# Mixture-of-experts blocks of 32 rows on four column tiles in place of 64 rows on two

## The reference, cut to what matters

```python
def expert_block(args):
    xb, e = args
    g, u = jnp.split(xb @ w_gu[e], 2, axis=-1)        # (rows,1024) @ (1024,1024)
    return (jax.nn.silu(g) * u) @ w_dn[e]             # (rows,512) @ (512,1024)
...
y = ys[dest].reshape(T, TOP_K, D)
return jnp.einsum('tk,tkd->td', wts.astype(y.dtype), y)
```

## Time and profile before

| | |
|---|---|
| median of 3 runs | 2094.38 us (2094.16 to 2096.64) |
| the profiled execution | 2094.28 us, its span 2092.5 us |
| PE busy | 1722.3 us, 82% of the span |
| DVE, ACT, POOL busy | 33%, 17%, 12% |
| moved by DMA | 516.19 MB, mean 247 GB/s |
| expert stage of layer 0 | from 459.86 to 1112.32 us |
| expert stage of layer 1 | from 1461.67 to 2064.68 us |

### The profile page before, as it was taken

How to read it: one execution, slowest core, us unless ns; L and a number is a source line. 1 busy time by engine, 2 the same in 40 slices (tenths; PEclk the granted TensorE clock), 3 DMA queues, 4 the chain that set the end, 5 groups by cost and what they waited for, 6 DMA issues and landing times.

```text
span 2092.5 us, 19483 instructions
## 1 busy us (share of the span) xinstructions
PE 1722.3 (82%) x7263; PEld 763.4 (36%) x7263; DVE 689.7 (33%) x1090; ACT 354.9 (17%) x740; POOL 250.1 (12%) x242
## 2 busy tenths in 40 slices
PE   3899999869596678788886999795969888888883
PEld 2545776443132223223323444344323332323231
DVE  5286554252212322211112279875111111111112
ACT  1234442101010101111101124310111111101110
POOL 1002110021211211111100111100011101110100
PEclk9999999959898889899997999895999999999997
DMA  9065000337959888999993412033695999999985
GB/s 374 11 249 193 0 0 1 122 148 268 411 211 394 355 355 343 387 359 370 358 350 137 153 60 73 8 150 143 223 386 217 363 365 356 363 354 359 350 346 202
DMA packets 144707, 516.19 MB, mean 247 GB/s; under 512 B 14738, under 2 KB 27215, under 8 KB 141299
## 3 DMA queue, kind: packets, MB, share of 16 engines
q1 hardware_dynamic: 128912, 497.96, 61.4%
q0 software_dynamic: 13408, 16.85, 2.3%
q10 hardware_dynamic: 2306, 0.28, 0.1%
HBM read 515.03 MB, written 29.36 MB: 260 GB/s over the span
## 4 chain that ended last, share of the span: by engine, by line
PE 62%; DMA 21%; DVE 12%; issue 2%; ACT 1%; SPq 1%; POOLq 0%; DVEq 0%; POOL 0%; ACTq 0%
PE ps L932 25%; DMA ring_gu<-in_moe_w_gu_dram 19%; PE ps L945 11%; PE ps L761 3%; PE ps L866 3%; PE ps L672 3%; PE ps L788 3%; PE ps L831 2%; DVE ring_dn L1566 2%; PE ps L687 2%; PE ps L774 1%; PE ps L707 1%; DVE gate_bc L1277 1%; DMA ring_gu<-in_w_ada_dram 1%; PE ps L938 1%
## 5 line engine op out<-in xcount | busy, mean ns | idle before, releaser
L932 PE MATMUL ps<-ring_gu,arena 128*64 128x512 f32 x2816 | 700.0, 643 | 199.5 <-DMA ring_gu<-in_moe_w_gu_dram 196.0
L932 PEld LDWEIGHTS ps<-ring_gu,arena 128*64 128x64 f32 x2816 | 208.3, 147 | 619.7 <-issue 530.2
L945 PE MATMUL ps<-ring_dn,arena 128*64 128x512 f32 x1408 | 317.1, 592 | 0.9 <-ACT arena L1214 0.9
L573 POOL DMA_INDIRECT ys_dram<-arena,out_idx x88 | 126.5, 1438 | 1077.3 <-DVE arena L1753 1077.3
L1777 DVE TENSOR_TENSOR arena<-arena,ps 128x256 f32<-128x256 f32 x88 | 37.0, 421 | 588.9 <-ACT arena L1227 588.9
L1214 ACT ACTIVATE arena<-ps 128x256 f32<-128x256 f32 x88 | 33.7, 384 | 849.1 <-PE ps L938 849.1
L945 PEld LDWEIGHTS ps<-ring_dn,arena 128*64 128x64 f32 x1408 | 100.9, 137 | 201.3 <-issue 199.9
L1753 DVE SCALAR_TENSOR_TENSOR arena<-ps,wtab,gate_bc 128x512 f32<-128x512 f32 x88 | 66.0, 751 | 237.1 <-PE ps L945 237.1
L1742 DVE TENSOR_SCALAR arena<-ps,scale_col,shift_col 128x128 f32<-128x128 f32 x176 | 60.1, 403 | 223.3 <-PE ps L923 223.3
L831 PE MATMUL ps<-arena 128*128 128x512 f32 x256 | 110.6, 592 | 1.0 <-ACT arena L1070 1.0
L1206 ACT ACTIVATE arena<-ps,shift_col,scale_col 128x128 f32<-128x128 f32 x176 | 66.2, 456 | 91.2 <-PE ps L923 91.2
(11 more groups left out here) (290 smaller groups left out, 1476.8 us busy)
## 6 DMA issues: line engine op xcount, KB each, us to landing
ring_gu<-in_moe_w_gu_dram SPq DMA_DIRECT2D x64, 4096.0 KB, 18.2
ring_dn<-in_moe_w_dn_dram SPq DMA_DIRECT2D x64, 2048.0 KB, 10.1
ring_gu<-in_w_ada_dram SPq DMA_DIRECT2D x12, 2048.0 KB, 10.3
arena<-in_w_ada_dram SPq DMA_DIRECT2D x16, 1536.0 KB, 11.2
ring_dn<-ys_dram SPq DMA_DIRECT2D x8, 1024.0 KB, 7.8
arena<-in_rnn_w_in_dram SPq DMA_DIRECT2D x8, 1024.0 KB, 5.8
ring_gu<-in_mla_w_o_dram SPq DMA_DIRECT2D x1, 4096.0 KB, 19.3
xn_dram<-arena SPq DMA_DIRECT2D x2, 2048.0 KB, 18.3
```

The lines of the kernel that those rows point to most:

```text
L573: g.indirect_dma_start(ys_dram, bass.IndirectOffsetOnAxis(ap=out_idx[:, col:col + 1], axis=0), yo[:, n % 2, :], None, bounds_check=4 * SEQ ...
L932: last = mm(ps[s_ * ROWS:(s_ + 1) * ROWS, pb, :].rearrange("p (a b) -> p a b", a=2), rows[:, k, :], pair[:, :, s_, :], start=(k == 0), sto ...
L945: last = mm(ps[s_ * ROWS:(s_ + 1) * ROWS, pb, :], part, w[:, f, s_ * HALF:(s_ + 1) * HALF], start=(f == 0), stop=(f == FT - 1))
```

## The change

`ROWS` becomes 32 and there are four column tiles (`TILES`). The caps are 2, 2, 5, 4, 3, 3, 3, then 2 for nine ranks and 1 for sixteen: 56 blocks. Ranks with 1 block alternate with the larger ones in `SEQUENCE`. In `gate_up` and `down` each matmul has a 128x32 stationary and a 128x256 moving operand, four to a slice. The hidden block is 128x128, so that one transpose does; the ACT and DVE operations on it are half as long, and a row of `yo` is 256 numbers, written to `ys_dram` in rows of 256. A unit is four blocks; the first unit is gathered with one indirect DMA, each other unit with four of 32 rows. The counting of blocks and columns in DVE takes a few more operations, the building of `tok_idx` fewer.

```diff
+QUARTER = D // 4
-ROWS = 64
-CAP = [2, 2, 4] + [2] * 7 + [1] * 22
+ROWS = 32
+TILES = P // ROWS
+CAP = [2, 2, 5, 4, 3, 3, 3] + [2] * 9 + [1] * 16
+SEQUENCE = [0, 1, 16, 2, 17, 3, 18, 4, 19, 5, 20, 6, 21, 7, 22, 8, 23, 9, 24, 10, 25, 11, 26, 12, 27, 13, 28, 14, 29, 15, 30, 31]
+BLOCKS = [(_o, _j) for _o in SEQUENCE for _j in range(CAP[_o])]
...
+                    for q in range(TILES):
+                        o, j = BLOCKS[TILES * t + q]
+                        col = o + COLBASE[j]
+                        rows = slice(q * ROWS, (q + 1) * ROWS)
+                        g.indirect_dma_start(xg[rows, t % 2, :], None, xn_dram,
+                                             bass.IndirectOffsetOnAxis(ap=tok_idx[0:ROWS, col:col + 1], axis=0),
...
                     for k in ks:
-                        pair = w[:, k, :].rearrange("p (two s f) -> p two s f", two=2, s=2)
-                        for s_ in range(2):
-                            last = mm(ps[s_ * ROWS:(s_ + 1) * ROWS, pb, :].rearrange("p (a b) -> p a b", a=2), rows[:, k, :],
-                                      pair[:, :, s_, :], start=(k == 0), stop=(k == KT - 1))
+                        parts = w[:, k, :].rearrange("p (two s f) -> p two s f", two=2, s=TILES)
+                        for s_ in range(TILES):
+                            last = mm(ps[s_ * ROWS:(s_ + 1) * ROWS, pb, 0:2 * P].rearrange("p (a b) -> p a b", a=2),
+                                      rows[:, k, :], parts[:, :, s_, :], start=(k == 0), stop=(k == KT - 1))
...
-                    if half and t + 1 < NU:
+                    if q == TILES - 1 and t + 1 < NU:
                         rows_transposed(t + 1)
...
-                then(v.tensor_scalar(ncap, order, float(HEAVY), 1.0, ALU.is_lt, ALU.add))
-                then(v.tensor_scalar(ovb, order, 2.0, 2.0, ALU.is_equal, ALU.mult))
-                then(v.tensor_tensor(ncap, ncap, ovb, ALU.add))
+                then(v.tensor_scalar(ovb, order, 2.0, float(NE), ALU.is_lt, ALU.mult))
+                then(v.tensor_tensor(ovb, ovb, order, ALU.add))
+                then(v.tensor_scalar(ncap, order, 16.0, 1.0, ALU.is_lt, ALU.add))
+                for first in (7.0, 4.0, 3.0):
+                    then(v.scalar_tensor_tensor(out=ncap, in0=ovb, scalar=first, in1=ncap, op0=ALU.is_lt, op1=ALU.add))
...
-                    v.scalar_tensor_tensor(out=yo[:, n % 2, :], in0=ps[:, 5 + n % 2, :], scalar=wtab[:, col:col + 1],
-                                           in1=gate_bc[:, 1, 0:HALF], op0=ALU.mult, op1=ALU.mult
+                    v.scalar_tensor_tensor(out=yo[:, n % 2, :], in0=ps[:, 5 + n % 2, 0:QUARTER], scalar=wtab[:, col:col + 1],
+                                           in1=gate_bc[:, 1, 0:QUARTER], op0=ALU.mult, op1=ALU.mult
```

More of the change, by code:

```diff
@@ L378, in dn_rows, with rows_landed @@
             return moe_w_dn[l, e].rearrange("(k p) n -> p k n", p=P)
+        def rows_landed(l, t):
+            return sum(16 if u == 0 else 16 * TILES for m in range(l + 1) for u in range(t % 2, NU, 2) if m < l or u <= t)
         @block.sync
@@ L586, in _ @@
                         gather(t + 2)
-                    if t:
-                        scatter(2 * t - 1)
-                    scatter(2 * t)
+                    for n in range(max(TILES * t - 1, 0), TILES * t + TILES - 1):
+                        scatter(n)
                 scatter(NB - 1)
@@ L960, in block_down @@
                         pe.wait_ge(S["yo_ready"], base + n - 1)
-                    down(5 + n % 2, hmidT[:, n % 2, :, :], DN[place % 2]).then_inc(S["dn_done"], 1)
+                    down(5 + n % 2, hmidT[:, n % 2, :], DN[place % 2]).then_inc(S["dn_done"], 1)
                 pe.sem_inc(OV[l]["dn_done"], 1)
@@ L1254, in _ @@
                         else:
-                            rows = slice(hf * ROWS, (hf + 1) * ROWS)
-                            A(gate_bc[rows, 1, 0:HALF], bank(g)[rows, :], ACT.Copy).then_inc(S["a_free"], 1)
+                            for q in range(2):
+                                rows = slice((2 * hf + q) * ROWS, (2 * hf + q + 1) * ROWS)
+                                last = A(gate_bc[rows, 1, 0:QUARTER],
+                                         bank(g)[rows, q * QUARTER:(q + 1) * QUARTER], ACT.Copy)
+                            last.then_inc(S["a_free"], 1)
         @block.vector
@@ L1446, in _ @@
                 else:
-                    rows = slice((n - 2) * ROWS, (n - 1) * ROWS)
-                    v.tensor_copy(gate_bc[rows, 1, 0:HALF], bank(g)[rows, :]).then_inc(S["d_free"], 1)
+                    for q in range(2):
+                        rows = slice((2 * n - 4 + q) * ROWS, (2 * n - 3 + q) * ROWS)
+                        last = v.tensor_copy(gate_bc[rows, 1, 0:QUARTER],
+                                             bank(g)[rows, q * QUARTER:(q + 1) * QUARTER])
+                    last.then_inc(S["d_free"], 1)
             def k_out(h, hb):
```

166 lines of the change are left out of this document (80 added, 86 removed).

## The result

The changed kernel takes **2007.5 us** (median of 4 runs, 2000.95 to 2008.95), beside 2094.4 before: ratio 0.9577, 95% interval 0.9554 to 0.9600. It is 87 us faster; 157 were forecast, and the range (1895 to 2030) held. The profiled execution took 2008.95 us, its span is 2007.2.

The account below looks back on a forecast made before the run. PE's time per block was taken to make holes in DMA, which would then bound the kernel. Gains of 16 (starts), 79 (layer 1) and 64 (layer 0), less 2 (DVE counting), made 157: 2094.3 to 1937 us, range 1895 to 2030.

Parts of the forecast that it names:

- Four at once: PE in gate_up and down: four column tiles run together, by the lower value for load-matmul pairs, giving a 5.7 us block.
- Rival 3: PE's expert blocks: two tiles at a time or pairs at 0.117 us, block about 11.1 us, 2161 us, slower; chance 0.11.
- DMA as the bound, holes only at large experts: Expert stages: weight transfers set the time, with holes of 12, 6 and three of 1 us, 21; layer 0 31.
- The slow half after a wait: PE after waiting for a load: runs at the half clock level, 2 us put into each larger expert's first block.
- Start of layer 1: First load comes 9.5 us after the first matmul, where it was 17.21; gain 7.7 us.
- 478.5 of transfers: Layer 1's expert stage: DMA moves the remaining bytes at 412 GB/s in 478.5 us.
- gathers hidden: POOL in the expert stages: 53 gathers for 22 a layer, about 1 us each, fit under 500 us and cost nothing.
- The loop isn't entered.: Overflow loop behind the blocks: the token counts fit the new caps, so no time was put in for it.
- 5 us from the last landing to the end of down: End of each expert stage: a down of 1.7 us and what is left of the last hidden block, 5 us.
- The start of layer 0: First load comes 9.5 us after the first matmul, where it was 18.04; gain 8.5 us.
- rival 2: PE's expert blocks: four tiles overlap only in part, block 8.5 to 9 us, 2010 to 2020 (1975 to 2060); chance 0.20.
- dearer scatters: Scatter rows of 1 KB in place of 2 KB: 12 us in both layers if dearer, kept only for the range.

Follow-up runs that it names:

- number 10: Number 9 with its one gather of 128 rows split again into four of 32, POOL's wait and DVE's copies kept; 1960.3 us.
- 11: number 10 without POOL's wait for DVE's column, the DVE copies kept but unused; 1972.0 us.
- Number 6: The changed kernel with fewer slices in gate_up and down from an expert's third block on, all loads kept, part of the computation left out; 1977.4 us.
- Number 9: The changed kernel with the overflow loop skipped by one outer condition and one gather of 128 rows per unit in place of four; 1934.2 us.
- number 1: The changed kernel with MAX_EXTRA, the trips of the empty overflow loop, back from 28 to 15; 1990.6 us.
- number 3: The changed kernel with each overflow loop inside one more condition, so that no trip is made; 1975.0 us.
- Number 8: The changed kernel with the second unit's gathers moved behind the accumulator's clearing and the load of b_ada on POOL; 2009.1 us.
- 2: The kernel before with only its overflow loops lengthened from 15 to 28 trips; 2110.6 us.
- number 4: The changed kernel with gate_up and down matmuls reordered: column tiles 0 and 1 over all slices, then 2 and 3; 2051.3 us.

## Why the prediction was right in kind and 70 us too low

Right, by its own steps:

- **Four at once.** The step that decided (a block of 5.7 us, by the lower bound for pairs) measured 5.8, and 5.57 without row transposes. Rival 3's premise and the Trainium skill's rule on weight loads ("TensorE: Matmul & The Clock Gate", "What overlaps and what doesn't") are refuted for column tiles: 32 loads with 32 matmuls start within 1.75 us, and a load lies under the matmuls of the other tiles.
- **DMA as the bound, holes only at large experts.** 13.3 us behind 5 blocks (forecast 12; but some 3 us of it are PE's short stops, as numbers 10 and 11 show, which the forecast didn't have). By the share in the second pair of windows, (1 - 0.98/1.02) x 523.7 = 20.5 us of holes in layer 1, where 21 stood in the sum; in layer 0 (1 - 0.97/1.02) x 581.5 = 28.5, where 31 stood. Number 6, which takes the large experts' work away, gives back 35 of these 49.
- **The slow half after a wait.** 3.64 us for 1.93, at the half level; with the second half 2.4 us, forecast 2. PE's mean clock fell to 0.85.
- **Start of layer 1.** 10.3 us, forecast 9.5.

By place, the 70.5 us between 1937 and 2007.5 are 19.5 and 25.2 in the two stages, 7.5 at their starts and 16.9 of trips, 69.1 together. By cause, in order of size, each by the run that isolates it, these terms were wrong:

- **"478.5 of transfers" at 412 GB/s, and gathers hidden.** The prediction priced the 53 gathers by POOL's time, which was indeed free (134 and 95 us busy), and took nothing for what they do to the weights' packets. Nor did it count that they stand ahead of `b_ada`, for which the first `hmid` waits. Between numbers 10 and 9 they cost 26.1 us, some 20 by the rate and 5.7 by that wait. Its last paragraph named loads below 400 GB/s as what would make it wrong; that is what happened (396 in the middle of layer 1's stage, where the share is full).
- **"The loop isn't entered."** It was priced at nothing because no trip has work, but the engines go through 28 trips in place of 15: 16.9 us (number 1). The full diff has `MAX_EXTRA`, and the 6.14 us "issue" ahead of the memset were in the trace of before; I read neither as a cost.
- **PE's short stops.** No term at all. 14.7 us between numbers 3 and 10 (10 also has DVE's copies and POOL's waits), and 11.7 between 11 and 10, the one beside 16.7 and the other beside 11.7 us of stops.
- **"5 us from the last landing to the end of down".** From the last landing, about 1961 and 1061, to the end of the last down are 9 us in either layer: the last expert's two loads land together, so nearly its whole `gate_up` with a slow half and two downs follow. That is 7.5 us in two layers. It is read from the windows; no run isolates it.

The four make 65.2 of 70.5; about 5 us stay open, if the parts add up as they stand. The start of layer 0 took 16.2 us, 6.7 more than the sum had, and is no fifth part: the wait for `b_ada` is in the 26.1. Its size is not fixed either: with the same gathers number 1 started in 12.2 us and number 10 in 17.7. Number 8 shows that removing this wait alone gains nothing, since the stops come in its place.

So the time fell where rival 2 had put it (1975 to 2060), and not by its mechanism: the tiles overlap in full. Number 9, which takes away what I had overlooked, gives 1934.2, the size that the sum had at 1937; but it also saves the 15.7 us of trips that the kernel before had, so the agreement is partly luck. That 2007.5 lies inside the range is luck in part too: the range was kept wide for partly overlapping tiles and for dearer scatters, not for what came.

## What to carry to other kernels

Price a DMA that you add by what it does to the others in flight, not by its issue alone: after a change that makes DMA the bound, look for windows where its share stays and its rate drops. A runtime loop costs its trips on every engine even when each is skipped, so put one condition around the whole. Once PE's work per buffer is short, short stops and a longer queue are no longer hidden, and the largest expert sets the holes.

## What the runs showed of the hardware that was not expected

- A trip of an empty runtime loop with one condition costs 0.74 us on PE (9.6 us for 13 trips in numbers 1 and 2, 20.7 for 28 in number 3) and 0.44 on POOL (5.8 us for 13; 0.57 at the end of layer 1 between number 1 and the changed kernel).
- Four indirect gathers of 32 partitions one behind the other take the weight loads from 412 to 291 GB/s in the window behind them, at a full share; one of 128 partitions with the same bytes does not.
- Matmuls on free column tiles start between those issued ahead of them on busy tiles: starts of L942 and L953 alternate within 0.04 us in number 4.
- PE can be stopped 0.3 to 1.0 us at a time, 1.0 to 2.1 us apart, with no wait open. It comes 1.7 to 7.0 us after the first of four indirect gathers in a row, also where DMA is nearly idle, and not in every program: one wait more for each unit on POOL (number 10) turned it off. The cause is open.
